# Encoder trunk on one core: memory rows transposed as they land, gain and rstd of the memory norm applied after the transposes and after the products

## What is computed

```
def rms_norm(x, g):
    y = x * lax.rsqrt(jnp.mean(x * x, axis=-1, keepdims=True) + EPS)
    return y * g

mem_n = rms_norm(mem, g_mem)                      # 256 x 1024, once
for l in range(DEPTH):                            # DEPTH = 2
    h = rms_norm(x, g_mix[l])                     # 256 x 1024
    ... h @ w_in[l] ...
    kv = (mem_n @ w_mem_kv[l]).reshape(b, n_mem, 2, 4, 128)
    k, v = kv[:, :, 0], kv[:, :, 1]               # memory keys and values
    ... attention of the layer's queries into k, v ...
```

## Time and profile before

| | us |
|---|---|
| three runs | 1714.0, 1713.49, 1714.32 |
| median | 1714.0 |
| span of the profiled execution, first to last instruction | 1711.3 |
| TensorE busy in it | 1695.4 (99%) |
| VectorE busy | 1338.2 (78%) |
| ScalarE busy | 1167.9 (68%) |
| GpSimd busy | 70.7 (4%) |
| DMA, mean over the span | 290 GB/s |

### The profile page before, as it was taken

One profiled execution on the slowest core, in us unless ns is written; L12 is line 12 of the kernel. 1 busy time (PEld: TensorE's weight loads), 2 busy tenths in 40 slices (PEclk: granted clock), 3 DMA queues, 4 the chain that ended last, 5 costly groups with the idle time before them and its releaser, 6 DMA issues.

```text
span 1711.3 us, 28291 instructions
## 1 busy us (share of the span) xinstructions
PE 1695.4 (99%) x9614; PEld 1476.0 (86%) x9614; DVE 1338.2 (78%) x1388; ACT 1167.9 (68%) x1362; POOL 70.7 (4%) x91
## 2 busy tenths in 40 slices
PE   9999999999999999999999999999999999999997
PEld 8988999999988989988888888888888888888886
DVE  7675575455457664779998989999899999899998
ACT  6565644444444655567888788787878887887876
POOL 4000000000000000020000000000000000000020
PEclk9999999999999999999999999999999999999999
DMA  9633468666646443699999999999999999999994
GB/s 346 184 111 113 144 231 302 181 194 184 185 160 205 124 113 111 220 363 393 383 370 391 380 372 397 365 388 392 365 386 385 359 395 380 373 398 370 382 350 164
DMA packets 169917, 496.57 MB, mean 290 GB/s; under 512 B 15584, under 2 KB 17680, under 8 KB 169344
## 3 DMA queue, kind: packets, MB, share of 16 engines
q1 hardware_dynamic: 165168, 480.57, 77.9%
q0 software_dynamic: 4688, 15.18, 2.7%
HBM read 482.56 MB, written 13.13 MB: 290 GB/s over the span
## 4 chain that ended last, share of the span: by engine, by line
PE 93%; ACT 3%; DVE 2%; issue 1%; DMA 0%; POOL 0%; DVEq 0%; ACTq 0%
PE ps L1873 87%; PE ps L2320 1%; ACT probs L1136 1%; PE ps L2136 1%; PE ps L2119 1%; PE ps L2106 1%; PE ps L2108 0%; ACT probs L1128 0%; PE ps L2327 0%; PE ps L1925 0%; DVE wlo L1342 0%; ACT whi L996 0%; DVE probs L1577 0%; DVE row_max L1555 0%; DVE probs L1550 0%
## 5 line engine op out<-in xcount | busy, mean ns | idle before, releaser
L1342 DVE TENSOR_TENSOR wlo<-raw,whi 128x1024 fp32r<-128x1024 f32 (+1 forms) x768 | 910.5, 1218 | 272.2 <-ACT whi L996 251.0
L996 ACT ACTIVATE whi<-raw 128x1024 fp32r<-128x1024 f32 (+1 forms) x768 | 800.5, 1057 | 311.7 <-PE ps L1873 298.6
L1873 PE MATMUL ps<-whi,xg_hi 128*128 128x512 f32 x896 | 352.2, 393 | 0.9 <-DVE xg_lo L1763 0.9
L1873 PE MATMUL ps<-wlo,xg_hi 128*128 128x512 f32 x896 | 349.4, 390 | 0.0
L1873 PE MATMUL ps<-whi,xg_lo 128*128 128x512 f32 x896 | 349.1, 390 | 0.0
L1873 PE MATMUL ps<-hT_hi,whi 128*128 128x256 f32 x896 | 259.5, 290 | 0.7 <-ACT gates L1006 0.7
L1873 PE MATMUL ps<-hT_lo,whi 128*128 128x256 f32 x896 | 253.9, 283 | 0.0
L1873 PE MATMUL ps<-hT_hi,wlo 128*128 128x256 f32 x896 | 253.8, 283 | 0.0
L1873 PEld LDWEIGHTS ps<-whi,xg_hi 128*128 128x128 f32 x896 | 168.3, 188 | 37.0 <-DVE wlo L1342 3.4
L1873 PEld LDWEIGHTS ps<-wlo,xg_hi 128*128 128x128 f32 x896 | 168.3, 188 | 35.1
L1873 PEld LDWEIGHTS ps<-whi,xg_lo 128*128 128x128 f32 x896 | 168.4, 188 | 33.9
(11 more groups left out here) (328 smaller groups left out, 2027.7 us busy)
## 6 DMA issues: line engine op xcount, KB each, us to landing
raw<-in_w_down_exp SPq DMA_DIRECT2D x216, 512.0 KB, 6.4
raw<-in_w_gate_exp SPq DMA_DIRECT2D x210, 512.0 KB, 5.7
raw<-in_w_up_exp SPq DMA_DIRECT2D x120, 512.0 KB, 5.7
raw<-in_w_in SPq DMA_DIRECT2D x72, 512.0 KB, 3.7
vM<-in_w_up_exp SPq DMA_DIRECT2D x56, 512.0 KB, 5.5
kM<-in_w_up_exp SPq DMA_DIRECT2D x48, 512.0 KB, 5.7
raw<-in_w_gate_dense SPq DMA_DIRECT2D x28, 512.0 KB, 4.0
raw<-in_w_up_dense SPq DMA_DIRECT2D x28, 512.0 KB, 3.7
```

The costliest lines, as they stand in the source:

```text
L996: s.activation(whi[n % SPLIT][:, 0:w], raw[tile(key)][:, 0:w], ACT.Copy).then_inc(chunk_hi, 1)
L1342: v.tensor_tensor(wlo[n % SPLIT][:, 0:w], raw[tile(key)][:, 0:w], whi[n % SPLIT][:, 0:w].bitcast(F32), ALU.subtract).then_inc(chunk_split, 1)
L1873: ins = mm(o, lhsT, rhs, start=start and i == 0, stop=stop and i == 2, skip_group_check=True)
```

## The change

The memory rows are transposed raw, as they land. `g_mem` is loaded as a column (eight DMAs of 128 x 1 numbers, issued by ScalarE's queue, `mem_gain`), and multiplied in per partition when ScalarE and VectorE take the transposed rows out of PSUM. rstd (`mem_rstd`) is applied to the results: to the values when they are copied out (two instructions in place of one), to the keys by a row vector `mem_rows`, which TensorE makes from two diagonal matrices (`rstd_rows`). `keys_out` moves from ScalarE to VectorE, for both layers. `mem_rows` (128 KB) is spilled and read back with the split memory. SP loads the first key chunk ahead of `mem`, and no longer the 512 KB of broadcast `g_mem`. The squares of the memory rows, their mean and rstd move behind the four key chunks' splits; on GpSimd the position loads and the mask come first, then rstd of the memory, then the load of `g_mix`, then the small loads. TensorE's spare matmuls become 9 and 4.

```diff
@@ SP @@
+            load(opening[0])
             for t in range(NT):
                 sp.dma_start(normed[:, t, :], A["mem"][0, P * t:P * (t + 1)]).then_inc(mem_loaded[t], 16)
-            sp.dma_start(gain[:, :], A["g_mem"].partition_broadcast(P)).then_inc(mem_gain_loaded, 16)
-            for key in opening[0:SPLIT]:
+            for key in opening[1:SPLIT]:
                 load(key)
...
+                if key == ("qa", 0, 3):
+                    wait_read(sp, ("mem_rows",))
+                    sp.dma_start(rows_spill, mem_rows[:, :]).then_inc(mem_saved, 16)
@@ GpSimd @@
-            rstd_of(0)
             for t in range(NT):
                 pool.dma_start(pos_i[:, t:t + 1],
...
+            rstd_of(0, mem_rstd)
+            load_gain(1, A["g_mix"][0])
             for l in range(DEPTH):
                 pool.dma_start(g_lat[:, l, 0:Q_RANK], A["g_q_lat"][l].partition_broadcast(P)).then_inc(small_loaded, 16)
...
             pool.dma_start(wr[:, :, :], A["w_router"][0].rearrange("(k p) e -> p k e", p=P)).then_inc(router_loaded, 16)
-            nc.gpsimd.memset(mask[:, :, :], 0.0).then_inc(constants, 1)
...
-            load_gain(1, A["g_mix"][0])
@@ ScalarE @@
+            for k in range(KD):
+                eng.dma_start(mem_gain[:, k:k + 1], A["g_mem"][P * k:P * (k + 1)].unsqueeze(1)).then_inc(mem_gain_loaded, 16)
+            hi_of(opening[0])
+            eng.wait_ge(mem_gain_loaded, 16 * KD)
+            for a in range(2):
+                wait_full(eng, ("memT", a, "area"))
+                for k in range(4 * a, 4 * (a + 1)):
+                    c = TOK * (k - 4 * a)
+                    ins = s.activation(memT_hi[:, k, :], ps[a][:, c:c + TOK], ACT.Copy, scale=mem_gain[:, k:k + 1])
+                    if k % 2:
+                        ins.then_inc(hi_copied, 1)
+                hi_of(opening[1 + a])
+            hi_of(opening[3])
             for t in range(NT):
                 eng.wait_ge(mem_loaded[t], 16)
                 for half in range(2):
                     square(normed, half, t)
...
-            transposed(("memT",), memT_hi)
...
-            keys_out(0)
@@ VectorE @@
             def values_out(l):
                 key = ("memv", l)
                 wait_full(eng, key)
-                v.tensor_copy(vM[:, l, :, :].rearrange("p t n -> p (t n)"),
-                              area(key)[:, :]).then_inc(psum_free[areas[key]], 1)
+                for t in range(NT):
+                    ins = v.tensor_scalar(vM[:, l, t, :], area(key)[:, 512 * t:512 * (t + 1)], mem_rstd[:, t:t + 1],
+                                          None, ALU.mult)
+                ins.then_inc(psum_free[areas[key]], 1)
+
+            def keys_out(l):
+                key = ("memk", l)
+                wait_full(eng, key)
+                v.tensor_tensor(kM[:, l, :, :], area(key)[:, :].rearrange("p (h n) -> p h n", h=M_HEADS),
+                                mem_rows[:, :].unsqueeze(1).to_broadcast([P, M_HEADS, TOK]),
+                                ALU.mult).then_inc(psum_free[areas[key]], 1)
...
-            norm(0, normed, normed)
-            for i, key in enumerate(opening[0:4]):
-                lo_of(key)
-                transposed_piece(("memT",), i, memT_hi, memT_lo)
+            v.memset(mem_ones[:, :], 1.0).then_inc(mem_ones_ready, 1)
+            lo_of(opening[0])
+            eng.wait_ge(mem_gain_loaded, 16 * KD)
+            for a in range(2):
+                for i in range(2 * a, 2 * (a + 1)):
+                    eng.wait_ge(hi_copied, tl.after("hi_copied", ("memT", i)))
+                    for k in range(2 * i, 2 * (i + 1)):
+                        c = TOK * (k - 4 * a)
+                        ins = v.scalar_tensor_tensor(memT_lo[:, k, :], ps[a][:, c:c + TOK], mem_gain[:, k:k + 1],
+                                                     memT_hi[:, k, :].bitcast(F32), ALU.mult, ALU.subtract)
+                    ins.then_inc(hT_split, 1)
+                lo_of(opening[1 + a])
+            lo_of(opening[3])
             reduced_angles()
-            for key in opening[4:6]:
-                lo_of(key)
+            for t in range(NT):
+                norm_mean(0, t)
+            lo_of(opening[4])
+            eng.wait_ge(constants, 3)
+            for t in range(NT):
+                eng.wait_ge(rstd_ready, t + 1)
+                v.tensor_scalar(mem_diag[:, t, :], ident[:, :], mem_rstd[:, t:t + 1], None, ALU.mult).then_inc(norm_done, 1)
+            lo_of(opening[5])
+            wait_full(eng, ("mem_rows",))
+            v.tensor_copy(mem_rows[:, :], area(("mem_rows",))[:, 0:TOK]).then_inc(psum_free[0], 1)
+            wait_read(eng, ("mem_rows",))
+            keys_out(0)
             wait_full(eng, ("memT", 1, "area"))
             norm(1, x, normed)
@@ TensorE @@
+            def rstd_rows():
+
+                key = ("mem_rows",)
+                wait_free(pe, key)
+                pe.wait_ge(mem_ones_ready, 1)
+                pe.wait_ge(norm_done, NT)
+                for t in range(NT):
+                    ins = mm(area(key)[:, P * t:P * (t + 1)], mem_ones[:, :], mem_diag[:, t, :], start=True, stop=True)
+                ins.then_inc(psum_full[0], 1)
...
-            keep_busy(27, ps[3][:, 0:P])
+            keep_busy(9, ps[3][:, 0:P])
             transposes(("memT",), 0)
-            keep_busy(7, ps[3][:, 0:P])
+            keep_busy(4, ps[3][:, 0:P])
...
                     mem_values(l, c)
+                    if l == 0 and c == 0:
+                        rstd_rows()
```

More of the change, by code:

```diff
@@ L180, in build_tally @@
     transposed(("memT",))
+    psum(("mem_rows",), 0)
     psum(("memk", 0), 2, full=chunks(mem_chunks("memk", 0)))
@@ L397, in trunk_kernel @@
         ang = sb("ang", [P, 5, NT, 48])
+        mem_gain = sb("mem_gain", [P, KD])
+        mem_rstd = sb("mem_rstd", [P, NT])
         meansq = sb("meansq", [P, NT])
@@ L572, in trunk_kernel @@
         mem_gain_loaded = sem("mem_gain_loaded")
+        mem_ones_ready = sem("mem_ones_ready")
         gain_loaded = sem("gain_loaded")
@@ L862, in _, with rstd_of @@
                                     pattern=[[-1, P]], channel_multiplier=1).then_inc(constants, 1)
-            def rstd_of(n):
+            def rstd_of(n, dst=rstd):
                 for t in range(NT):
                     pool.wait_ge(meansq_ready, NT * n + t + 1)
-                    nc.gpsimd.tensor_tensor(rstd[:, t:t + 1], meansq[:, t:t + 1], power[:, 0:1],
+                    nc.gpsimd.tensor_tensor(dst[:, t:t + 1], meansq[:, t:t + 1], power[:, 0:1],
                                             ALU.pow).then_inc(rstd_ready, 1)
-            rstd_of(0)
             for t in range(NT):
@@ L874, in _ @@
             pool.dma_start(freqs[:, :], inv_freq.partition_broadcast(P)).then_inc(positions_loaded, 16)
-            for l in range(DEPTH):
-                pool.dma_start(g_lat[:, l, 0:Q_RANK], A["g_q_lat"][l].partition_broadcast(P)).then_inc(small_loaded, 16)
-                pool.dma_start(g_lat[:, l, Q_RANK:], A["g_kv_lat"][l].partition_broadcast(P)).then_inc(small_loaded, 16)
-                pool.dma_start(sink[:, l, :], A["sink"][l].partition_broadcast(P)).then_inc(small_loaded, 16)
-            pool.dma_start(wr[:, :, :], A["w_router"][0].rearrange("(k p) e -> p k e", p=P)).then_inc(router_loaded, 16)
             nc.gpsimd.memset(mask[:, :, :], 0.0).then_inc(constants, 1)
@@ L887, in _ @@
                                     base=0, pattern=[[1, P]], channel_multiplier=-1).then_inc(constants, 1)
+            rstd_of(0, mem_rstd)
             load_gain(1, A["g_mix"][0])
+            for l in range(DEPTH):
+                pool.dma_start(g_lat[:, l, 0:Q_RANK], A["g_q_lat"][l].partition_broadcast(P)).then_inc(small_loaded, 16)
+                pool.dma_start(g_lat[:, l, Q_RANK:], A["g_kv_lat"][l].partition_broadcast(P)).then_inc(small_loaded, 16)
+                pool.dma_start(sink[:, l, :], A["sink"][l].partition_broadcast(P)).then_inc(small_loaded, 16)
+            pool.dma_start(wr[:, :, :], A["w_router"][0].rearrange("(k p) e -> p k e", p=P)).then_inc(router_loaded, 16)
             for l in range(DEPTH):
@@ L1028, in _ @@
                     square(normed, half, t)
-            for key in opening[0:2]:
+            for key in opening[4:6]:
                 hi_of(key)
-            def keys_out(l):
-                copy_out(("memk", l), kM[:, l, :, :].rearrange("p h n -> p (h n)"), area(("memk", l))[:, :])
-            transposed(("memT",), memT_hi)
-            for key in opening[2:6]:
-                hi_of(key)
+            eng.wait_ge(meansq_ready, NT)
             eng.wait_ge(x_loaded, 16)
@@ L1040, in _ @@
                     square(x, half, t)
-            hi_of(opening[6])
-            keys_out(0)
-            hi_of(opening[7])
+            for key in opening[6:]:
+                hi_of(key)
             eng.wait_ge(angles_ready, 1)
@@ L1648, in _ @@
                 if l == 0:
-                    for key in dense_first[2:SPLIT]:
-                        lo_of(key)
```

(9 more changed lines are left out.)

19 lines of the change are left out of this document (10 added, 9 removed).

## The result

| | before | after |
|---|---|---|
| median of the runs, us | 1713.97 (6 runs, 1713.49 to 1714.32) | 1719.31 (6 runs, 1718.71 to 1719.86) |
| span of the profiled execution, us | 1711.3 | 1717.2 |
| TensorE busy in it, us | 1695.4 | 1695.2 |
| mean granted clock of TensorE | 0.999 | 0.997 |

The changed kernel is slower: ratio 1.0033, 95% interval [1.0023, 1.0043], so +5.3 us, with 3.9 to 7.4 as its interval. The profiled execution's own time is 1718.92, 1.7 over its span. TensorE has as much work as before; what is lost is lost ahead of the first `qa` matmul. Its weight load stands at 43.49 us, against 37.12, a shift of 6.4 us.

What follows compares the result with a forecast made beforehand. TensorE was taken as the bound from its first key matmul at 13.05 us. Profiled span 1711.3, plus shift 3.7 (t0 - 6.3 with t0 = 10.0), plus 2.7 outside the span, gave 1717.7 us; range 1713.4 to 1720.6.

Steps and rivals of the forecast that it cites:

- the shift: Delay of the first `qa` matmul, passed one to one to the end: t0 - 6.3, so +3.7 us.
- t0: Moment when the gain column and the first transposes of the memory are both there: forecast 10.0 us.
- VectorE's row: VectorE's rests, splits, angles, mean squares and diagonals after t0, now the long one: ends at t0 + 14.3.
- the load of `g_mix`: GpSimd issues it after the second diagonal, at t0 + 14.3; with the median 7.4 us it lands at t0 + 21.7.
- TensorE waiting for x: After value chunk 2 TensorE idles 3.3 us until half 0 of x is normed, at t0 + 23.0.
- three signs: Wrong if `memT_hi` starts at 8 or 12, norm of x waits for rstd, or first `qa` shift differs from the end's.
- The front: Opening loads and transposes: second half of `mem` lands at 7.5 us, half of its transposes fill PSUM area 0 by 8.0.
- the column comes later: Rival: column packets each wait for one of SP's queue; t0 = 11.8, +5.5 us, 1719.5; chance 0.26.
- From t0 to the first key matmul: ScalarE takes two pieces, VectorE two rests; TensorE starts at t0 + 1.5 = 11.5 us.
- The clock: Slower TensorE after its idle 3.3 us ahead of x: 1.1 us, put in the range only, on top of each rival.
- The other side: Rival: TensorE keeps its head start and never waits for x; t0 = 8.0, -3.5 us, 1710.5; chance 0.06.

Runs made afterwards that it cites:

- the version with rows: Changed kernel with the gain column made on the chip: g_mem loaded as 8 rows in one DMA, transposed by TensorE, copied out by VectorE; 1717.30 us.
- the kernel with 18 steps: Changed kernel with 18 spare steps in place of 4 on TensorE ahead of the first key matmul; 1719.87 us.
- The reordered kernels: Gain by rows, early `g_mix`, VectorE reordered, then angles' second half and sine later, rstd of x earlier: 1711.35 us; with the spill behind the `qa` chunks too: 1711.21.
- the kernel in which SP holds back: Changed kernel, but SP issues three loads, then waits until the eight gain column loads have landed before issuing more; 1720.47 us.
- the reordered version: Changed kernel with gain by rows, early `g_mix`, norm of x ahead of the row vector's copy and keys' way out, angles cut in two; 1714.43 us.
- the one with 38 spare steps: Changed kernel with 38 spare steps in place of 4 on TensorE ahead of the first key matmul; 1720.47 us.

## Why the prediction was right, and where it was not

Forecast 1717.7, measured 1719.31, inside the range and slower than before by 0.31%. The direction was right, and so was the way the shift is made up: t0, VectorE's row, the load of `g_mix`, TensorE waiting for x. The term t0 was not, and of the three signs that I had named for being wrong two came: `memT_hi` starts at 12.76, and the norm of x waits for rstd and not for the gain. How near the sum came is in part luck, as said below.

- **The front.** `mem`'s second half came at 8.65 and not at 7.5, its transposes of area 0 end near 9.3. In the version with rows, without the column's packets, it comes at 7.6, so the column takes 1 us from the loads beside it. It did not matter, since the column was later still.
- **t0, the step that failed.** Forecast 10.0, by the row of eight columns issued by GpSimd; measured 12.76. Two parts: the last issue stands at 4.66 and not at 3.95 (ScalarE's issues took 0.50 and up to 0.75 us, SP's 0.43), and the loads took up to 8.1 us. I had the right mechanism as the rival "the column comes later", at 11.8, and gave it less weight because the rows of GpSimd spoke against it. The turn-by-turn count was right where both queues had work (199 packets to 199 from 9 to 10 us). Its bound was 1.0 us short: there were 128 packets more than the 1024 that I had counted, the column's last packet started near 12.2, and it landed 0.6 behind that.
- **From t0 to the first key matmul.** Forecast 1.5, measured 1.9: an instruction of 256 columns with a scale is not the 0.38 of the earlier trace rows; two of ScalarE take 0.85 and two of VectorE 0.89 in the chain.
- **VectorE's row.** The second diagonal starts at t0 + 14.5 and ends at t0 + 14.8 (forecast for the end: 14.3); 0.25 of it is a wait for `mem_rstd`, which I had left out. The steps by duration, of rows that stood in the trace, hold to 0.5 us over 14.
- **The load of `g_mix`.** 6.4 us where I took the median 7.4; it was issued 0.8 after the second diagonal was due, at t0 + 15.1, and landed at t0 + 21.5 (forecast 21.7). The two errors cancel, which is luck. That this load holds the norm of x was right only in part: rstd stood at t0 + 21.7, since TensorE's keys were slow, where I had 20.1; that it ended so near to my 21.7 is luck again. With full clock the load is alone in holding it (35.06, waiting 2.45 us for it).
- **The clock.** I put 1.1 us of it in the range, behind the idle time ahead of x. It came in another place, behind the wait for the column, and cost 2.3 us of TensorE's time and nothing of the end, because the load of `g_mix` covers it. Ahead of x TensorE was idle for 1.35 us and not 3.3, for the same reason, and kept its clock there. Where it is idle for 3.04 us, in the version with rows, the term is real and 1.2 us; where it is idle for 3.38 us, in the kernel with 18 steps, the granted clock stays at 1.00 and the term is nothing. The rule of the Trainium skill, TensorE: Matmul & The Clock Gate, Part 1, that an idle engine falls to 1.2 GHz, agrees with the granted 0.50 behind the column and in the version with rows, and the kernel with 18 steps does not show it. The 1.1 us that I would have added by it were not in this kernel's sum.
- **The shift.** t0 - 6.3 gives +6.5 with the measured t0, and the profile has +6.4 at the first `qa`. At 198, 268, 298 and 681 us it is 6.4 still; the span is 5.9 longer and the median 5.3. The last 0.5 goes near 750 us, in a part that the change does not touch: VectorE's queue loads a number that the program needs, L1756 before and L1801 now.

```profile
748.86 0.92 DVEq L1756
```

```profile
755.22 0.43 DVEq L1801
```

In the twelve other kernels this step took 0.42 to 0.88 us, so it is chance and no gain of the change. What lies around the span is 1.7 in the profiled execution, where I had taken 2.7 from before. With the measured t0 the forecast's own sum is 1711.3 + 6.5 + 2.7 = 1720.5, only 0.1 inside the range; these two terms, which have nothing to do with the change, brought the measured time further in.
- **The other side.** That the head start is kept needed `g_mix` within 2 us and 3 us less of VectorE's row. The reordered kernels did just these two, and came out at 1711.2, near its 1710.5; the changed kernel itself had no way there.

## What to carry to other kernels

A load of many tiny pieces is priced by the number of its packets beside the packets of the queue that runs next to it, not by its bytes: load such a vector as a few rows and turn it on the chip. A queue of its own did not help here, since SP's queue beside it was full. Where two or three branches end within a fraction of a microsecond of each other, an edit to one of them can give next to nothing, as here (0.4 us at most), and only both together show what they are worth. And an opening that is made shorter must be followed to the next queue: here the gain column, then the norm's own gain, then VectorE's order, then the spill in front of the next weights.

## What the runs showed of the hardware

- Where both had work waiting, two hardware queues got packets through one for one: 199 to 199 and 197 to 198 in a microsecond, at 4 bytes against some 2 KB. Without the neighbour 663 of the same packets went in 0.4 us.
- In the kernel in which SP holds back, the column's last packet started before 7.6 us, and the column landed at 9.40: at least 1.8 us between the two. In the changed kernel it is 0.6 us (near 12.2, and 12.76), so this distance is not a fixed one. What sets it is not shown.
- A granted clock of 0.50 stayed for some 5 us of unbroken matmuls behind an idle 3.9 us, and for some 3 us behind an idle 3.0; behind idle times of 1.35 us it was 1.00, and behind the 1.95 us of the reordered version the matmuls took 0.63 us in place of 0.39. In one kernel of the same opening (the one with 38 spare steps) it was at 0.50 from 9 to 11 us behind waits of 0.76 and 1.09 us, and in the one with 18 it stayed at 1.00 behind an idle 3.38, so the length of the idle time alone does not tell. The fall can also come after the work has begun again: in the version with rows TensorE resumed at 32.25 and the granted clock was 1.00 until 33.
- The same load, `g_mix` by GpSimd with 512 KB, took 6.4, 6.5, 6.6, 6.7, 7.1 and 7.3 us in the six kernels that issue it in this place: a spread of 0.9 us, and in four of them this load is what the norm of x waited for last.
